# Hybrid mLSTM / RG-LRU / GLA step on one core: value pairs last in both projections, the first head loaded before the stage ends, output banks squared one by one

## What is computed

```python
# layer A (even)
proj = rmsnorm(x) @ w_in_a             # q, k, v, og, gates, z, xr, gr
hm   = sigmoid(og) * mlstm(q, k, v, gates)      # 4 heads, a 256 x 256 state each, chunked
hm   = head_norm(hm) * silu(z)
hl   = rglru(conv(xr)) * silu(gr)
x    = x + rmsnorm(concat(hm, hl) @ w_out_a)
# layer C (odd)
proj = rmsnorm(x) @ w_in_c             # q, k, v, r, low-rank gate
o    = head_norm(gla(q, k, v, gate)) * silu(r)  # 4 heads, a 256 x 512 state each, chunked
x    = x + rmsnorm(o @ w_out_c)
```

## Time and profile before

| | us |
|---|---|
| median of 3 runs (2181.13 to 2185.22) | 2181.74 |
| profiled execution | 2187.39 |
| its span, first to last instruction | 2185.7 |
| PE busy in it | 2051.1 |
| POOL busy in it | 275.7 |
| mean granted TensorE clock, of 1 | 0.968 |

### The profile page before, as it was taken

The page is one execution under the profiler, slowest core; times in us unless marked ns, Lnnn a source line. Parts: engine busy times, 40 slices in busy tenths (PEclk is TensorE's granted clock), DMA queues, the critical chain, the costliest instruction groups (busy, mean ns, idle before and its releaser), DMA issues. The chain is left out here.

```text
span 2185.7 us, 32847 instructions
## 1 busy us (share of the span) xinstructions
PE 2051.1 (94%) x12590; PEld 1841.3 (84%) x12590; DVE 1324.1 (61%) x2299; ACT 843.7 (39%) x1536; POOL 275.7 (13%) x384
## 2 busy tenths in 40 slices
PE   5999999999999589999958999999999699999997
PEld 4999999999999478788738999999999577777774
DVE  5456676555456666666646556655666585666664
ACT  5455543332232444444344444222223344334333
POOL 3000000000000211121121000000000243323322
PEclk8999999999999799999978999999999799999999
DMA  2112133343332645555331322444233444544442
GB/s 101 56 64 63 63 112 90 118 157 94 105 101 79 220 128 165 154 158 164 97 135 44 103 85 80 134 151 128 86 113 100 170 150 166 177 164 171 172 149 69
DMA packets 209222, 264.36 MB, mean 121 GB/s; under 512 B 48228, under 2 KB 156004, under 8 KB 207032
## 3 DMA queue, kind: packets, MB, share of 16 engines
q1 hardware_dynamic: 209080, 262.42, 38.0%
HBM read 172.39 MB, written 89.99 MB: 120 GB/s over the span
## 5 line engine op out<-in xcount | busy, mean ns | idle before, releaser
L547 DVE TENSOR_TENSOR pa_stage<-pa_ps,pa_stage 128x536 f32<-128x536 f32 x110 | 77.0, 712 | 129.9 <-PE pa_ps L514 124.4
L547 DVE TENSOR_TENSOR pc_stage<-pc_ps,pc_stage 128x536 f32<-128x536 f32 x110 | 77.0, 712 | 105.3 <-PE pc_ps L514 93.9
L362 PE MATMUL pa_ps<-a_XT_hi,pa_w_hi 128*128 128x358 f32 x576 | 133.1, 339 | 0.3 <-PEq L197 0.3
L362 PE MATMUL pa_ps<-a_XT_hi,pa_w_lo 128*128 128x358 f32 x576 | 126.0, 327 | 0.0
L362 PE MATMUL pa_ps<-a_XT_lo,pa_w_hi 128*128 128x358 f32 x576 | 125.7, 326 | 0.0
L514 PE MATMUL pc_ps<-c_XT_hi,pc_w_lo 128*128 128x268 f32 x384 | 110.2, 287 | 0.0
L514 PE MATMUL pc_ps<-c_XT_hi,pc_w_hi 128*128 128x268 f32 x384 | 110.2, 287 | 0.0
L514 PE MATMUL pa_ps<-a_XT_hi,pa_w_lo 128*128 128x268 f32 x384 | 110.1, 287 | 0.0
L514 PE MATMUL pc_ps<-c_XT_lo,pc_w_hi 128*128 128x268 f32 x384 | 110.1, 287 | 0.0
L514 PE MATMUL pa_ps<-a_XT_lo,pa_w_hi 128*128 128x268 f32 x384 | 110.1, 287 | 0.0
L514 PE MATMUL pa_ps<-a_XT_hi,pa_w_hi 128*128 128x268 f32 x384 | 109.9, 286 | 0.0
(11 more groups left out here) (542 smaller groups left out, 6153.1 us busy)
## 6 DMA issues: line engine op xcount, KB each, us to landing
pa_w_raw<-in_w_a SPq DMA_DIRECT2D x57, 512.0 KB, 4.6
pc_w_raw<-in_w_c SPq DMA_DIRECT2D x49, 512.0 KB, 4.7
scr_c<-pc_stage SPq DMA_DIRECT2D x48, 512.0 KB, 3.2
scr_a<-pa_stage SPq DMA_DIRECT2D x40, 512.0 KB, 3.2
ma_hin<-scr_a SPq DMA_DIRECT2D x32, 512.0 KB, 3.4
mc_hin<-scr_c SPq DMA_DIRECT2D x32, 512.0 KB, 3.7
mc_sample_state<-in_s SPq DMA_DIRECT2D x32, 512.0 KB, 4.5
out_s_s<-mc_sample_state SPq DMA_DIRECT2D x32, 512.0 KB, 2.9
```

The lines of the kernel that those rows point to most:

```text
L362: ins = pe.matmul(self.ps[:, 3 * s + t, 0:TC], w[:, k, :], x[:, k, t * TC:(t + 1) * TC], start=(k == 0 and j == 0), stop=(k == KT - 1 and ...
L547: dve.tensor_tensor(dst, self.out(p, product), x, ALU.add).then_inc(self.added, 1)
```

## The change

1. The pairs are made in another order. A: k, og, z, v (was k, v, og, z). C: r, v (was v, r). The last four (eight) pairs are thus values, which have no gate and are spilled straight after DVE's add.
2. Before the spills of the last pair but one are issued, SP loads what the mix needs for its first head into a buffer that outlives the projection (`S.head`, `FirstHead.load`). The buffer serves the projection as scratch before that, for the token sums and the sigmoids.
3. The projection's SP no longer waits for its spills at the end. The mix waits where it reads: SP before it loads the second head (`projected(1)`) and the fourth (`projected(3)`), ACT before its loop.
4. `m_used` gets an extra count when the first output bank of a chunk is complete, and `post_act` and `tail_act` wait for each bank by itself.
5. In the mix of A, DVE updates the head's state first, and makes the numerator and the division behind it.
6. In the mix of C, SP loads the first sample state ahead of the gain and the residual.

```diff
...
-        sp.dma_start(self.G.raw[s][:], self.G.w_d[self.first + 2 * p + s]).then_inc(self.loaded[s], 16)
+        sp.dma_start(self.G.raw[s][:], self.G.w_d[self.tiles[p] + s]).then_inc(self.loaded[s], 16)
...
+A_KINDS = ("k", "og", "z", "v")
+A_SPILLED = [32 * (4 + 12 + h + 1) for h in range(H)]
...
-        temps = a.sb("pa_t_temps", [P, 3, HC])
+        temps = S.head[:, 0:3 * HC].rearrange("p (k t) -> p k t", t=HC)
...
+                    if p == NPAIR - 2:
+                        sp.wait_ge(z_read, 2 * H)
+                        for s in range(2):
+                            sp.wait_ge(spilled[s], A_SPILLED[0])
+                        load_first_head(sp)
...
                 sp.wait_ge(lru_spilled, 16 * 2 * 8)
-                for s in range(2):
-                    sp.wait_ge(spilled[s], 16 * 2 * 20)
                 sp.wait_ge(finished, 96)
...
+            if half == 0 and last:
+                ins.then_inc(self.m_used, 1)
         return ins
+
+    def used(self, n):
+
+        return n + 1 + (n + 1) // H
...
     def post_act(self, act, ps, c, junk):
-        act.wait_ge(self.m_used, 4 * c + 4)
         for half in range(2):
+            act.wait_ge(self.m_used, self.used(4 * c + 3) - 1 + half)
             act.activation(junk, ps[:, 6 + half, :], ACT.Square, accum_out=self.stat[:, half:half + 1]).then_inc(self.squares, 1)
...
     def tail_act(self, act, ps, buf):
-        act.wait_ge(self.m_used, 4 * NC)
         for half in range(2):
+            act.wait_ge(self.m_used, self.used(4 * NC - 1) - 1 + half)
...
+class FirstHead:
...
+    def load(self, sp):
+        sp.dma_start(self.hin, self.scr_d[0, 0, :, 0:8, :]).then_inc(self.hin_in, 16)
+        if self.row_d is not None:
+            sp.dma_start(self.row, self.row_d[0:1, 0:P].to_broadcast([P, P])).then_inc(self.hin_in, 16)
+        sp.dma_start(self.samples, self.scr_d[8, 0, :, 0:8, TAIL:LAST]).then_inc(self.samples_in, 16)
+        if self.row_d is not None:
+            sp.dma_start(self.z, self.scr_d[0, 0, :, 8:10, :]).then_inc(self.z_in, 16)
...
-                load_head(0)
-                load_sample_head(0)
+                def projected(h):
+                    for s in range(2):
+                        sp.wait_ge(S.spilled[s], A_SPILLED[h])
+                projected(1)
                 load_head(1)
                 load_hl(0)
-                load_z(0)
                 load_state(0)
                 O.load_late(sp)
+                projected(3)
                 O.load_post(sp, post_d)
...
                 part_a(0)
+                for s in range(2):
+                    act.wait_ge(S.spilled[s], A_SPILLED[3])
                 for n in range(NSTEP):
...
                 for n in range(NSTEP):
                     c, h, rows = where(n)
                     u = unit_of(n)
+                    dve.wait_ge(b_done, n + 1)
+                    update(cst[:, h, :, :], S.wc[:, h, c:c + 1]).then_inc(state_ready, 1)
                     part_num(n)
                     divide(linker(dve, den_chain, 3 * n), sm, num, S.tok[0:rows, c, 2, h:h + 1], og, gg).then_inc(gated_ready, 1)
-                    dve.wait_ge(b_done, n + 1)
-                    update(cst[:, h, :, :], S.wc[:, h, c:c + 1]).then_inc(state_ready, 1)
...
```

More of the change, by code:

```diff
@@ L1495, in stage_mix_a @@
         O = OutRing(S, a, "ma", w_early, w_late, OUT_ORDER_A, 0, x_d, y_d)
-        hin = [a.sb(f"ma_hin{s}", [P, 8, P]) for s in range(2)]
-        zin = [a.sb(f"ma_z{s}", [P, 2, P]) for s in range(2)]
-        row = [a.sb(f"ma_row{s}", [P, P]) for s in range(2)]
+        hin = [first.hin, a.sb("ma_hin1", [P, 8, P])]
+        zin = [first.z, a.sb("ma_z1", [P, 2, P])]
+        row = [first.row, a.sb("ma_row1", [P, P])]
         hl = a.sb("ma_hl", [P, 8, P])
@@ L1512, in stage_mix_a @@
         sm = a.sb("ma_small", [P, 8])
-        hs_in = [a.sb(f"ma_sample_in{s}", [P, 8, NS]) for s in range(2)]
+        hs_in = [first.samples, a.sb("ma_sample_in1", [P, 8, NS])]
         zs_in = [a.sb(f"ma_sample_z{s}", [P, 2, NS]) for s in range(2)]
@@ L1569, in stage_mix_a @@
         pool_chain = sem("ma_pool_chain")
-        hs_loaded = [sem(f"ma_sample_in_loaded{s}") for s in range(2)]
+        hs_loaded = [first.samples_in, sem("ma_sample_in_loaded1")]
         zs_loaded = [sem(f"ma_sample_z_loaded{s}") for s in range(2)]
@@ L2501, in stage_mix_c @@
         O = OutRing(S, a, "mc", w_early, w_late, list(range(16)), 1, x_d, y_d)
-        hin = [a.sb(f"mc_hin{s}", [P, 8, P]) for s in range(2)]
+        hin = [first.hin, a.sb("mc_hin1", [P, 8, P])]
         rin = a.sb("mc_rin", [P, 4, P])
@@ L2512, in stage_mix_c @@
         sm = a.sb("mc_small", [P, 8])
-        hs_in = [a.sb(f"mc_sample_in{s}", [P, 8, NS]) for s in range(2)]
+        hs_in = [first.samples, a.sb("mc_sample_in1", [P, 8, NS])]
         rs_in = a.sb("mc_sample_r", [P, 4, NS])
@@ L2528, in stage_mix_c @@
         ps = a.ps("mc_ps", [P, 8, 512])
-        hin_in = [sem(f"mc_hin_in{s}") for s in range(2)]
+        hin_in = [first.hin_in, sem("mc_hin_in1")]
         r_in = sem("mc_r_in")
@@ L2549, in stage_mix_c @@
         pool_chain = sem("mc_pool_chain")
-        hs_loaded = [sem(f"mc_sample_in_loaded{s}") for s in range(2)]
+        hs_loaded = [first.samples_in, sem("mc_sample_in_loaded1")]
         rs_loaded = sem("mc_sample_r_loaded")
@@ L2893, in _ @@
                         aux_copy(0, j - 1)
+                for s in range(2):
+                    act.wait_ge(S.spilled[s], C_SPILLED[3])
                 for n in range(NSTEP):
@@ L3143, in build_program @@
             S.rrow = la.sb("rrow", [H, T])
+            S.head = la.sb("first_head_a", [P, 13 * P])
+            S.spilled = [S.a.sem(f"pa_spilled{s}") for s in range(2)]
+            first = FirstHead(S, scr_a, scr_r, "ma")
             raw_rows = ExitStack()
@@ L3162, in build_program @@
             S.gf = lc.sb("gf", [P, 8, 17])
+            with ExitStack() as gate_rows:
+                S.alow = make_alloc(nc, gate_rows).sb("pc_alow", [LOWK, TP], F32R)
+            S.head = lc.sb("first_head_c", [P, 10 * P])
+            S.spilled = [S.a.sem(f"pc_spilled{s}") for s in range(2)]
             scr_c = nc.dram_tensor("scr_c", [NC, H, P, CF, P], F32, kind="Internal").ap()
+            first = FirstHead(S, scr_c, None, "mc")
             raw_rows = ExitStack()
```

126 lines of the change are left out of this document (71 added, 55 removed).

## The result

The changed kernel takes **2170.11 us** (median, 2169.74 to 2172.95) against 2182.48 (2181.13 to 2185.22) of the kernel before beside it: a ratio of **0.9939, interval 0.9924 to 0.9953**, 12.4 us less. A second measurement on another chip gave 0.9933 (0.9920 to 0.9947). Faster, as forecast, but the forecast was 21.1 us less, and 2170.1 lies outside its range.

What follows compares the result with a forecast made beforehand. PE, busy 2051.1 of 2185.7 us, was taken as the bound; -9.7 + 1.3 - 0.7 + 3.2 - 9.5 - 0.5 - 0.5 - 4.7 = -21.1 us from the median 2181.74 gave 2160.6 us, range 2155 to 2167.5.

Steps and rivals of the forecast that it cites:

- Passages: Change from projection to mix: PE starts earlier in A, -9.7 us; the block starts earlier in C, -4.7 us.
- Chunk changes: Seven chunk changes of A's mix: PE's waits for the state (6.2) and an output bank (3.3) go, -9.5 us.
- The state first: A's mix, steps 0 to 3: the update ahead of the numerator delays each step by 0.79 us, +3.2 in all.
- The ordinary steps: A's mix from step 4 on: the later quotient is covered by 1.62 us of slack, so 0 change.
- First steps: Steps 0 to 8 of A's mix: +2.2 us, being 1.3 - 0.7 + 3.2 less 1.6 of the first chunk change.
- The late third head: Start of A's mix: head 2 lands behind the late weights and PE waits for it, +1.3 us (0 to 2.6).
- Clock: First steps of A's mix: the shorter gap may keep PE's clock at 2.4 GHz, half of 1.45 taken, -0.7 us.
- Transfers taking the place of the waits: Rival, chance 0.16: in A's mix head 2 comes 4.9 us late, late weights or z cost a microsecond more; 2165.2 us.
- The clock that stays up: Rival, chance 0.12: A's steps 0 and 1 gain 1.45 + 1.0 us and no transfer is late; 2157.5 us.
- the rival without it: Rival, chance 0.06: the early block does not come and both passages keep 4 to 5 us; 2170.1 us.
- The quotient: Rival, chance 0.02: the delayed quotient lengthens each of 32 later steps of A's mix by 0.79 us; 2195.4 us.
- Tails: Ends of A's and C's mix: ACT's first copy runs under PE's last four products, -0.5 us each.

Runs made afterwards that it cites:

- experiment 9: Changed kernel with DVE's clearing of C's state moved behind its first work on head 0, PE no longer waiting for it: 2167.18 us, ratio 0.9914.
- Experiment 6: Changed kernel with the samples' quotient (steps 9, 17, 25, 33 of A's mix) behind the product with z: 2169.84 us, ratio 0.9925.
- the passages alone: Changed kernel without state first and with both banks squared together, leaving order of pairs, first head and spill waits: 2173.41 us, ratio 0.9950.
- experiment 1: Changed kernel with DVE's old order in A's mix, numerator and quotient before the state: 2166.69 us, ratio 0.9903.
- the DVE edits alone: Kernel before with only the state first on DVE and the banks squared singly: 2184.67 us, ratio 0.9991.
- experiment 7: Changed kernel with the state first only at head 1 of each later chunk of A's mix, quotient first elsewhere: 2168.99 us, ratio 0.9923.
- experiments 1 and 2: The first is experiment 1; the second is the changed kernel with the state first only from step 4 on: 2168.76 us, ratio 0.9913.

## Why the prediction was wrong

**Passages: right.** -9.86 and -4.96 against -9.7 and -4.7. The block's end no longer waits for a landing, A's head is there, and C's early head gives nothing, for the reason given: experiment 9 frees it and gets 2.0 to 5.5 us.

**Chunk changes: the step that failed.** It says "So both lines of the earlier trace rows go: 6.2 + 3.3 = 9.5", with bounds of -9.5 and -6. Both lines did go. But steps 8 to 35 gave 3.6 instead of 7.9. The four combinations of the two edits in that stretch, each within 0.1 where it was repeated (but for the 282.23 above; the 283.3 has 0.6 of clock in it):

| | quotient first | state first | state first, samples' quotient behind |
|---|---|---|---|
| banks together | 281.6 | 283.3 | |
| banks singly | 277.0 | 278.1 | 274.9 |

Without the clock's part the banks were worth 4.6 in both columns, more than the 2.8 that their waits in this stretch add up to (six of 0.43 and one of 0.19); where the rest comes from, no run shows. The state first cost 1.1 in both rows instead of giving 5.3 (six waits of 0.89). Cut step by step, it gave 0.65 at each of the three chunk changes without sample work (steps 13, 21 and 29) and lost 0.77 at each of the four with it (9, 17, 25 and 33). The ordinary steps kept their time (from step 8 to step 9 it is 9.75 us in every profile), as forecast. The waits of the earlier trace rows were read as PE's loss; they were also DVE's slack. In steps 9, 17 and 25 DVE has the samples' sum and quotient to do ahead of the product with z, and the step can't end before that. In step 9 the 0.9 us that PE waited for the state, 6.1 us into the step, it now waits 11.6 us into it for the product with z (1.06), and 0.26 in between for the sample state. "What is late next is the sample state" names the smaller half; the product with z was not looked at. Experiment 6 moves one instruction group and gets 3.3 back.

**First steps: the late head mis-sized, the rest mixed with the clock.** For steps 0 to 8 the forecast was +2.2; it came to +3.2 against the mean of the four profiles, to +1.3 against the one that the forecast was read from (96.37) and to +3.9 against the three later ones (93.8). The late third head was put at +1.3; its wait was 1.9 to 2.0 in the changed kernel, 2.8 with the passages alone and 3.0 in experiment 1, and the time from step 1 to step 2 became 2.6 longer. The state first was sized right for one step (from step 3 to step 4 14.6 became 15.4, 0.8 as forecast), but in sum it was 0.5 to 2.9 us by the experiments, not 3.2: a part lies under the wait for the head, and the rest can't be told from the clock. Nor do the parts add. Against the later profiles the passages alone cost 3.8 in this stretch (97.56), the DVE edits alone 4.2 (97.99), both together 3.9 (97.63); against the first one 1.2, 1.6 and 1.3. How much of that is overlap and how much is clock stays open.

**Clock: wrong in place and sign.** The -0.7 was about step 0, which became 0.3 shorter (6.14 instead of 6.41 us): the clock fell all the same, 1.6 us into the block, with a mean of 0.93 from 712 to 714 us and 0.50 from there to 720. Not thought of were two dips later: 0.57 from 775 to 779 us behind the wait of step 3, and the one at A's end, 1.5 us.

```profile
775.00:779.00 4.00, 4.00 (x14) 3.17 (x13) 1.29 (x3) 0.94 (x2) 0.73 (x1) 0.57 0.81 195
```

The dip at A's end was there in every profile of the changed kernel and in none of the kernel before; the dips in C's mix moved from one profile of the changed kernel to the next. The Trainium skill, "TensorE: Matmul & The Clock Gate", Part 1, says that the moment of a change differs from run to run; the traces of C's mix agree, those of A's end do not show it.

**Rivals.** Transfers taking the place of the waits: true in kind (the third head, 1.9 us), not in size. The clock that stays up did not come. The early block came in both layers; that the rival without it gives 2170.1, the very time that was measured, is chance. The quotient did not set PE's pace in ordinary steps: experiment 7 has the quotient first there, and the same 278.2 us from step 8 on. But in the steps with sample work it was this mechanism that decided, and the slack of 1.62 in the earlier trace rows was read from a step without it.

**Tails.** C's second copy starts 0.92 after its first and the tail is 0.48 shorter, as forecast. In A, DVE's add behind the copies ends 1.95 us after PE's last product instead of 2.43, also 0.48 less; the stretch to C's norm (-0.10) varies by 2 us and hides it. One reading was off without harm: between the last products of the two banks lie eighteen products (twelve of the second half, six for the sample state), not six. C's copies:

```profile
2161.38 0.59 ACT L1466 ACTIVATE first_head_c<-mc_ps 48x512 f32<-48x512 f32 x1 [3.78 <-PE mc_ps L1421]
2162.30 0.59 ACT L1466 ACTIVATE first_head_c<-mc_ps 48x512 f32<-48x512 f32 x1 [0.33 <-PE mc_ps L1421]
```

Squaring banks singly, and the passages, carry the gain: 4.6 and 14.8 us. What takes from it are the first steps, the state first together with the samples' quotient, and 1.5 us of clock. What stays open: 1 to 3 us in the other stretches, which is what they vary by, the cause of the dip, what state first costs the first steps, and why experiments 1 and 2 are some 3 to 4 us better by their ratios than their stretches say.

## What to carry to other kernels

A wait of the bounding engine is its loss only down to the next chain that ends in the same step: before counting it, look at the step's last product and what the other engine has in front of it, in the very steps where the wait falls, not in an ordinary one. Where two waits share a chain, their prices need not add, and a late transfer can hide the cost of a reordering until it is mended. Moving work that nobody waits for behind the work that somebody waits for gave 3.3 us (four small instructions) and 2.0 to 5.5 us (one clearing); a forecast that rests on one execution should know how its stretches vary from one to the next, and a stretch should be compared only together with its granted clock: the kernel before took 73.5 us from step 0 to step 6 of A's mix in one execution and 70.7 in another.

## What the hardware showed that was not expected

A stretch of 27 steps in which DVE and PE alternate repeats within 0.1 us on different chips (the changed kernel: 278.15, 278.11, 278.10), and the one execution that does not (282.23) has a dip of the granted clock in it, while a stretch fed by loads ("C's norm") varied from 46.98 to 49.80. Single dips of the granted clock near the end of a mix cost 0.7 to 1.5 us each. Some keep their place: at A's end the clock fell in the same four microseconds in each profile of the changed kernel and in none of the kernel before, for 1.5 us. Others move: in C's mix the changed kernel had one between 2120 and 2130 us in one profile, one between 2140 and 2150 in another and none at either place in the third, and behind the wait in step 3 of A the clock fell in one of four executions of the kernel before, for 2.9 us with the longer wait.
